# A decoder step on one core: the next step's keys transposed ahead of a step's exponential, with three slots for the memory tokens

## The chip, the cores and the metric

The kernel runs on one core of a Trainium2 chip. The metric is the device time of one execution in microseconds; lower is better. The engines are named as in the profile: PE (TensorE, matrix products and transposes) with PEld (its weight loads), DVE (VectorE), ACT (ScalarE), POOL (GpSimd) and SP (SyncE, which here only issues DMAs). All numbers are float32.

## The reference, cut to what matters

One layer of a decoder is computed for a prompt of 512 tokens and a sample group of 8 sequences with 4 new tokens each. The part that the change touches is the attention of the sample group, and what runs beside it.

```
# latent attention of the sample group over a paged cache of 2048 tokens
q_lat  = einsum('bthd,chd->bthc', q_nope, w_uk)
s_past = (einsum('bthc,bkc->bhtk', q_lat, lat_past)
          + einsum('bthr,bkr->bhtk', q_rope, kr_past)) * scale
p      = softmax(concat([s_past, s_new]))
o_lat  = einsum('bhtk,bkc->bthc', p[..., :P], lat_past) + ...
o      = einsum('bthc,chd->bthd', o_lat, w_uv)

# attention of the sample group into 256 memory tokens, 4 heads
s = einsum('bthd,bmhd->bhtm', q, mem_k) * X_HEAD_DIM ** -0.5
o = einsum('bhtm,bmhd->bthd', softmax(s), mem_v)

# expert layer: 128 experts for each of 544 tokens, rows gathered from two tables
a   = gelu(einsum('cd,ckd->ck', h, peer_u[idx]))
out = einsum('ck,ckd->cd', gate * a, peer_v[idx])
```

`lat_past` and `kr_past` are gathered by `page_table`: 8 sequences with 16 pages of 128 tokens; a page is 128 KB of latents and 16 KB of rotary keys.

## The kernel before

Tokens are taken in five tiles: four of 128 prompt tokens and one with the 32 sample tokens. The first 550 us compute projections and prompt attention, and end with the expert choice of tiles 0 and 1. From then on POOL issues one indirect DMA after another: 128 rows of `peer_u`, one for each expert place of a tile, then 128 of `peer_v`, in the order u0, v0, u1, v1, u2 and so on (`gather_order`; 1088 gathers of 512 KB). Their targets are a ring of 12 buffers. DVE reduces each u row with one custom instruction (`products`), PE adds up the v rows four at a time (`weigh`). A u gather waits for the row 12 places before it to be consumed.

Beside these gathers runs the background: `sample()` (the attention of the sample group, then its memory attention) and `part(1)` (merge of the branches, output projection, expert queries for tiles 2, 3 and 4). It is cut into units, and `background_ticks()` gives each unit a place in the order of gathers. DVE runs a unit when it has consumed the row that is 4 places ahead (`LAG`). PE and ACT have no other work in u0 and u1, so they run through their units there as fast as semaphores let them; in v0 PE runs them between quads of v rows. Everything of the background has to be over on PE before it starts on v1.

The paged attention has 16 steps (`STEPS`): four sequences and two pages each, 8 pages a step. A step s is, on the engines:

- SP and POOL load its pages into slot s % 3 (`load_pages`). SP issues five pages (ten DMAs) and POOL three. From step 3 on both wait first for the products with the values of step s - 3, which read the same slot (`pv_mm`). POOL does this in its queue of gathers, in front of gather 9 + 5 s.
- PE transposes the pages (`page_turns`, L689, 18 transposes in five groups over two banks), ACT copies each group out (L1211).
- PE makes the scores (`page_scores`, L937 and L941), DVE the running maximum (`largest`, L1695 to L1703), ACT the exponential (L1388), PE the transposed probabilities (`page_probs`, L689) and the product with the pages as values (`page_values`, L975), DVE adds it to the sum (`gather_values`, L1719 and L1720).

The program order on PE before the change, three units a step:

```
page_turns(s) | page_probs(s-1), page_scores(s) | page_values(s-1)
```

and on ACT: copies of `page_turns(s)` | copy of the probabilities of s - 1 | exponential of s. DVE has `largest(s)` in the second unit and `gather_values(s-1)` in the third. The memory attention has the same form with two units for each of 8 sequences, and loads of 1 MB into two slots (`load_memory`).

`pick` on DVE chooses experts for a head pair of a tile; in u0 it runs ahead of rows 0, 32 and 64. ACT waits in its own order for a pick's result (`picked_exp`) before it goes on with the background.

Of the kernel before, what the change touches and what calls it, by code (L numbers as in the profile page):

```python
# [13 lines left out]
P = 128  # L14
# [4 lines left out]
NB = 8  # L19
# [168 lines left out]
def hybrid_step(nc, x_prompt, x_sample, cache_lat, cache_kr, state_pool, cache_mk, cache_mv, page_table,  # L188
# [8 lines left out]
    with ExitStack() as ctx:  # L197
# [101 lines left out]
        wuvs = at(181, [2, 512])  # L299
# [3 lines left out]
        smem = [at(a, [2, 2, 512]) for a in (163, 172)]  # L303
# [75 lines left out]
        ld_smem = [sem(f"ld_smem{i}") for i in range(2)]  # L379
# [35 lines left out]
        def _(sp):  # L415
# [109 lines left out]
            def load_memory(b):  # L525
                if b < 2:
                    sp.wait_ge(pv_mm, STEPS - 2 + b)
                else:
                    sp.wait_ge(mo_mm, b - 1)
                    sp.wait_ge(mt_mm, 2 * (b - 1))  # L530
                for k, src in enumerate((cache_mk, cache_mv)):
                    sp.dma_start(smem[b % 2][:, k], src[0, b].rearrange("(m p) h e -> p m (h e)", p=P)).then_inc(
                        ld_smem[b % 2], 16)

            def load_merge(g, n):
# [6 lines left out]
                elif n < 3:  # L542
                    sp.wait_ge(mo_mm, (NB - 1, NB, NB)[n])
                    sp.wait_ge(mt_mm, 2 * NB)
                else:
                    sp.wait_ge(so_mm, 1)
                    sp.wait_ge(mo_mm, NB)
# [84 lines left out]
        def _(pool):  # L632
# [10 lines left out]
            def load_pages(s):  # L643
# [4 lines left out]
                for j, k in own_pages(s)[1]:  # L648
                    n = (4 * a + j) * PAGES + g * PGRP + k
                    page = pool.value_load(pagetab[0:1, n:n + 1], min_val=0, max_val=cache_lat.shape[1] - 1)  # L650
# [7 lines left out]
            for s, (kind, p, n) in enumerate(ORDER):  # L658
# [4 lines left out]
                if (s - 9) % 5 == 0 and 2 <= (s - 9) // 5 < STEPS:  # L663
                    load_pages((s - 9) // 5)
                if s == 124:
# [20 lines left out]
        def _(pe):  # L686
# [302 lines left out]
            def mem_turns(b):  # L989
                pe.wait_ge(ld_smem[b % 2], 32 * (b // 2 + 1))  # L990
                for i in range(2):
                    if b >= 1:
                        pe.wait_ge(mt_ev, 2 * b - 1 + i)
                    for k in range(4):
                        h, m = 2 * i + k // 2, k % 2
                        last = turn(bank[:, 4 + i, k * P:(k + 1) * P],
                                    smem[b % 2][:, 0, m, h * XD:(h + 1) * XD], P)
# [27 lines left out]
            def mem_values(b):  # L1025
# [3 lines left out]
                for m in range(2):  # L1029
                    for h in range(XH):  # L1030
                        last = pe.matmul(bank[32 * h:32 * h + TS, 7, 256:256 + XD], smpT[:, m, 32 * h:32 * h + TS],
                                         smem[b % 2][:, 1, m, h * XD:(h + 1) * XD], start=(m == 0), stop=(m == 1))
                last.then_inc(mo_mm, 1)

            def sample():

                pe.wait_ge(pq_ev, QJ)
                pe.wait_ge(sc_ev, QJ)
                for s in range(STEPS + 1):
                    if s == HALVES + 1:  # L1040
                        page_out(0)
                    if s < STEPS:
                        page_turns(s)
                    yield
# [22 lines left out]
                yield  # L1067
                pe.wait_ge(bank_zero, 2)
                for n in range(NB + 2):
                    if n >= 2:  # L1070
                        mem_out(n - 2)
                    if n < NB:
                        mem_turns(n)
                    if 1 <= n <= NB:
                        mem_probs(n - 1)
                    yield
                    if n < NB:
                        mem_scores(n)
                    if 1 <= n <= NB:
# [120 lines left out]
        def _(act):  # L1200
# [152 lines left out]

            def sample():

                act.wait_ge(id_next, 2)
                for s in range(STEPS + 1):
                    a, g = s // HALVES, s % HALVES
                    if s < STEPS:
                        for u in range(5):  # L1360
                            act.wait_ge(pt_mm, 5 * s + u + 1)
                            if s >= 1:
                                act.wait_ge(ps_mm, s)
                            src = bank[:, 4 + (5 * s + u) % 2]
                            if u < 4:
                                copy(latT[:, u].rearrange("p a b -> p (a b)"), src).then_inc(pt_ev, 1)
                            else:
                                copy(ropT[:], src[:, 0:PGRP * P]).then_inc(pt_ev, 1)
                    yield
                    if s >= 1:  # L1370
# [5 lines left out]
                        copy(probT.rearrange("p a b -> p (a b)"), bank[:, 7, 0:PGRP * P]).then_inc(pp_ev, 1)  # L1376
                    yield
# [17 lines left out]
                yield  # L1395
                for n in range(NB + 2):
                    if n < NB:
                        for i in range(2):
                            act.wait_ge(mt_mm, 2 * n + i + 1)
                            if n >= 1:  # L1400
                                act.wait_ge(ms_mm, n)
# [614 lines left out]
```

## Time and profile before

| | us |
|---|---|
| median of 3 runs (2405.80 to 2407.64) | 2406.39 |
| the profiled execution's own time | 2412.29 |
| its span, first to last instruction | 2410.6 |

The engines' busy shares of the span are PE 56%, DVE 47%, POOL 45%, ACT 13%. These are averages over stages with different limits; the rows below read the stages one by one.
### The profile page before, as it was taken

The page shows a single profiled execution, that of the slowest core. Times are in us where ns is not written, and L with a number is a line of the kernel's source. Part 1 is how long each engine was busy: PE and PEld are TensorE (multiplying, and loading weights), DVE is VectorE, ACT ScalarE, POOL GpSimd, SP SyncE. Part 2 cuts the span into 40 slices and gives each one's busy share as a digit, 9 for nine tenths or more (in the row PEclk, how much of TensorE's full clock was granted, in tenths as well). Part 3 has the DMA queues.
Part 4 walks back from the last instruction along what each step waited for, and adds up shares of the span by engine and source line. Part 5 has one row for each costly group of instructions (what it writes and reads, how often), then busy time and mean ns, then how long its engine had stood idle before and what let it go on. Part 6 is the DMA issues. An engine that isn't in the chain of part 4 may idle for free.

```text
span 2410.6 us, 22105 instructions
## 1 busy us (share of the span) xinstructions
PE 1353.5 (56%) x7122; PEld 803.3 (33%) x7122; DVE 1138.8 (47%) x2797; ACT 302.5 (13%) x760; POOL 1082.1 (45%) x1182
## 2 busy tenths in 40 slices
PE   7998999894454347998743855500045510034513
PEld 5874788783232224555531611100001100001100
DVE  2104521136757743434798074078866068840060
ACT  2214520112222121001010110000000000000000
POOL 0000000005564534555466156666666676666673
PEclk9998899996776658999865876655566755567656
DMA  6212045437786979999999579999999999999996
GB/s 197 76 57 59 1 111 147 147 107 273 252 293 223 362 277 364 353 370 374 345 389 402 180 275 364 362 391 372 373 345 353 370 384 379 369 348 358 371 384 258
DMA packets 328363, 688.02 MB, mean 285 GB/s; under 512 B 39943, under 2 KB 179528, under 8 KB 328239
## 3 DMA queue, kind: packets, MB, share of 16 engines
q0 software_dynamic: 160032, 576.69, 63.6%
q1 hardware_dynamic: 168215, 109.90, 15.7%
q8 instruction: 58, 0.95, 0.2%
q14 instruction: 58, 0.48, 0.1%
HBM read 682.36 MB, written 4.18 MB: 285 GB/s over the span
## 4 chain that ended last, share of the span: by engine, by line
PE 34%; DVE 23%; issue 12%; another core or an unknown queue 11%; DMA 8%; POOL 5%; DVEq 3%; ACT 2%; SPq 2%; POOLq 0%; ACTq 0%
PE bank L693 26%; DVE arena L1883 15%; POOL arena L640 5%; DVEq L1819 3%; PE bank L1175 3%; PE bank L689 2%; DMA arena<-in_w_mla_out_dram 2%; DMA arena<-in_peer_v_dram,arena 2%; DMA arena<-in_cache_mem_v_dram 1%; DMA arena<-in_x_sample_dram 1%; PE bank L1150 1%; DMA arena<-in_w_pool_out_dram 1%; ACT arena L1211 1%; DVE arena L1826 1%
## 5 line engine op out<-in xcount | busy, mean ns | idle before, releaser
L640 POOL DMA_INDIRECT arena<-in_peer_u_dram,arena x544 | 514.9, 947 | 842.1 <-PE bank L693 548.1
L693 PE MATMUL bank<-arena 128*128 128x256 f32 (+7 forms) x2940 | 706.1, 397 | 103.1 <-issue 52.0
L640 POOL DMA_INDIRECT arena<-in_peer_v_dram,arena x544 | 516.2, 949 | 405.6 <-PE bank L1175 159.3
L1883 DVE CUSTOM_DVE_ANT_0 arena<-arena,bank 128x1024 f32<-128x1024 f32 x544 | 639.2, 1216 | 58.5 <-issue 50.8
L693 PEld LDWEIGHTS bank<-arena 128*128 128x128 f32 (+2 forms) x2940 | 539.2, 192 | 270.2 <-issue 103.5
L1175 PE MATMUL bank<-arena 128*32 128x512 f32 x2176 | 383.4, 842 | 317.5 <-DMA arena<-in_peer_v_dram,arena 251.4
L689 PE MATMUL bank<-arena 128*128 128x128 f32 (+5 forms) x774 | 150.3, 344 | 586.3 <-DVE arena L1900 367.2
L689 PEld LDWEIGHTS bank<-arena 128*128 128x128 f32 (+5 forms) x774 | 115.0, 176 | 636.2 <-DVE arena L1900 368.4
L1175 PEld LDWEIGHTS bank<-arena 128*32 128x32 f32 x2176 | 80.3, 136 | 597.9 <-issue 597.8
L1211 ACT ACTIVATE arena<-bank 128x256 f32<-128x256 f32 (+12 forms) x399 | 156.6, 428 | 505.1 <-PE bank L693 143.5
L1912 DVE TENSOR_TENSOR arena<-arena,bank 128x1024 f32<-128x1024 f32 x5 | 6.1, 1221 | 380.7 <-PE bank L1175 194.8
L1215 ACT ACTIVATE arena<-arena 128x1024 f32<-128x1024 f32 (+5 forms) x27 | 22.6, 838 | 532.8 <-DVE arena L1912 405.3
L1787 DVE TENSOR_TENSOR arena<-arena,bank 128x256 f32<-128x256 f32 (+1 forms) x32 | 14.0, 437 | 155.5 <-PE bank L693 125.3
L1430 ACT ACTIVATE arena<-bank 128x256 f32<-128x256 f32 (+1 forms) x48 | 19.1, 398 | 305.8 <-PE bank L693 209.0
L1823 DVE MAX8 arena<-arena 128x8 f32<-128x128 f32 (+1 forms) x102 | 34.5, 338 | 36.4 <-ACT arena L1211 29.0
L1485 ACT ACTIVATE arena<-arena 128x128 f32<-128x128 f32 (+1 forms) x5 | 1.5, 293 | 397.8 <-remote 397.7
L651 POOL DMA_DIRECT2D arena<-in_cache_kv_latent_dram x42 | 23.5, 560 | 60.0 <-issue 59.9
L1883 DVE DVE_READ_ACCUMULATOR2_ANT arena<- 128x1 f32 x544 | 44.4, 82 | 4.3 <-issue 4.1
L1785 DVE TENSOR_TENSOR arena<-arena,bank 128x256 f32<-128x256 f32 (+1 forms) x16 | 7.0, 438 | 81.0 <-PE bank L693 64.8
L1150 PE MATMUL bank<-arena 128*128 128x128 f32 (+1 forms) x160 | 28.7, 290 | 24.6 <-issue 23.8
L1826 DVE MAX8 arena<-arena 128x8 f32<-128x128 f32 (+1 forms) x102 | 34.6, 339 | 8.7 <-issue 1.3
L1900 DVE TENSOR_TENSOR arena<-arena 128x128 f32<-128x128 f32 (+1 forms) x5 | 1.4, 273 | 77.9 <-ACT arena L1485 68.0
(142 smaller groups left out, 777.2 us busy)
## 6 DMA issues: line engine op xcount, KB each, us to landing
arena<-in_w_in_dram SPq DMA_DIRECT2D x48, 512.0 KB
arena<-in_w_peer_q_dram SPq DMA_DIRECT2D x32, 512.0 KB
arena<-in_cache_kv_latent_dram SPq DMA_DIRECT2D x86, 128.0 KB
arena<-in_peer_u_dram,arena POOLq DMA_INDIRECT x544
arena<-in_peer_v_dram,arena POOLq DMA_INDIRECT x544
arena<-in_w_o_dram SPq DMA_DIRECT2D x8, 1024.0 KB
arena<-in_w_in_dram SPq DMA_DIRECT2D x6, 1024.0 KB
arena<-in_cache_kv_latent_dram POOLq DMA_DIRECT2D x42, 128.0 KB
```

Of the source, the lines that this page charges most:

```text
L640: pool.indirect_dma_start(out=ring[s % RING], out_offset=None, in_=table[0], in_offset=IndirectOffsetOnAxis(ap=ix, axis=0)).then_inc(land[ ...
L651: pool.dma_start(lat[i][:, j, k], cache_lat[0][DynSlice(page, 1)].rearrange("a p c -> (a p) c")).then_inc(ld_pagp[i], 16)
L689: return pe.transpose(dst, src, eye[0:n, 0:n])
L693: last = pe.matmul(dst, lhs(k), rhs(k), start=(k == 0), stop=(k == n - 1))
L1150: last = pe.matmul(bank[0:n, 6 + i % 2, t * P:(t + 1) * P], qp[:, i % 2, t * P:t * P + n], keysT[:, i % 2], start=True, stop=True)
L1175: last = pe.matmul(bank[32 * j:32 * j + 32, c], zw[:, 32 * j + i], ring[at_slot[j] % RING][:, c * 512:(c + 1) * 512], start=(i == 0), stop ...
L1211: return act.activation(dst, src, ACT.Copy, scale=scale)
L1215: link(act.activation(junk[0:r, 0:width], src, ACT.Square, accum_out=ss[0:r, col:col + 1]))
L1819: dve.drain()
L1823: step(dve.max(values[:, 0:8], source))
L1826: step(dve.max(values[:, 8:16], source))
L1883: dve.tensor_tensor_reduce(ring[s % RING], ring[s % RING], h_dot, 1.0, 0.0, ALU.mult, ALU.add, act_a[:, p % 2, k:k + 1]).then_inc(u_free, 1)
```

## The change

`page_turns(s + 1)` and its copies move into the unit between `page_scores(s)` and `page_values(s - 1)` on PE, and on ACT ahead of the exponential of step s. The same is done in the memory attention, which gets a third slot of 1 MB. `w_uv` for the sample group moves to another address and is loaded after the third memory load instead of at step 1. SP issues six pages of a step and POOL two, whose numbers POOL now reads with one load; both keep three page slots and the same wait. The units of the paged attention get 6 rows a step instead of 5, and the later units move with them: the memory attention starts at tick 113 instead of 96, the merge goes from 160 to 268 instead of 138 to 260, the last parts in u1 start 6 rows later. The first loads of the merge get their waits anew.

```
-    return (mine, []) if s < 2 else (mine[0:5], mine[5:])
+    return (mine, []) if s < 2 else (mine[0:6], mine[6:])
...
-    ticks = [u0 + 3 + 5 * i // 3 for i in range(3 * (STEPS + 1))]
-    ticks += [u0 + 90 + 2 * i for i in range(3)]
-    ticks += [u0 + 96 + 2 * i for i in range(2 * (NB + 2))]
-    ticks += [u0 + 138 + 13 * h // 5 for h in range(2 * MERGE)]
-    ticks += [u1 + 11 + 2 * r for r in range(12)]
-    ticks += [u1 + 37 + 2 * t for t in range(3)]
-    ticks += [u1 + 44 + 5 * t // 2 for t in range(3)]
-    ticks += [u1 + 52 + 3 * j for j in range(QJ + 2)]
+    ticks = [u0 + 3 + 2 * i for i in range(3 * (STEPS + 1))]
+    ticks += [u0 + 106 + 2 * i for i in range(3)]
+    ticks += [u0 + 113 + 9 * i // 4 for i in range(2 * (NB + 2))]
+    ticks += [u0 + 160 + 23 * h // 10 for h in range(2 * MERGE)]
+    ticks += [u1 + 17 + 2 * r for r in range(12)]
+    ticks += [u1 + 43 + 2 * t for t in range(3)]
+    ticks += [u1 + 50 + 5 * t // 2 for t in range(3)]
+    ticks += [u1 + 58 + 14 * j // 5 for j in range(QJ + 2)]
...
-        smem = [at(a, [2, 2, 512]) for a in (163, 172)]
+        smem = [at(a, [2, 2, 512]) for a in (163, 171, 179)]
...
             def load_memory(b):
-                if b < 2:
-                    sp.wait_ge(pv_mm, STEPS - 2 + b)
+                if b < 3:
+                    sp.wait_ge(pv_mm, (STEPS - 2, STEPS - 1, STEPS - 1)[b])
                 else:
-                    sp.wait_ge(mo_mm, b - 1)
-                    sp.wait_ge(mt_mm, 2 * (b - 1))
+                    sp.wait_ge(mo_mm, b - 2)
+                    sp.wait_ge(mt_mm, 2 * (b - 2))
...
             for s in range(STEPS):
                 load_pages(s)
-                if s == 1:
-                    sp.dma_start(wuvs[:], w_uv[0].rearrange("(k p) h e -> p k (h e)", p=P)).then_inc(ld_wuv, 16)
             for b in range(NB):
                 load_memory(b)
+                if b == 2:
+                    sp.wait_ge(ps_mm, STEPS)
+                    sp.dma_start(wuvs[:], w_uv[0].rearrange("(k p) h e -> p k (h e)", p=P)).then_inc(ld_wuv, 16)
...
-                if (s - 9) % 5 == 0 and 2 <= (s - 9) // 5 < STEPS:
-                    load_pages((s - 9) // 5)
+                if (s - 9) % 6 == 0 and 2 <= (s - 9) // 6 < STEPS:
+                    load_pages((s - 9) // 6)
...
             def sample():
...
+                page_turns(0)
                 for s in range(STEPS + 1):
                     if s == HALVES + 1:
                         page_out(0)
-                    if s < STEPS:
-                        page_turns(s)
-                    yield
                     if s >= 1:
                         page_probs(s - 1)
                     if s < STEPS:
                         page_scores(s)
+                    yield
+                    if s + 1 < STEPS:
+                        page_turns(s + 1)
                     yield
                     if s >= 1:
                         page_values(s - 1)
                     yield
...
+                mem_turns(0)
                 pe.wait_ge(bank_zero, 2)
                 for n in range(NB + 2):
                     if n >= 2:
                         mem_out(n - 2)
-                    if n < NB:
-                        mem_turns(n)
                     if 1 <= n <= NB:
                         mem_probs(n - 1)
-                    yield
                     if n < NB:
                         mem_scores(n)
+                    yield
+                    if n + 1 < NB:
+                        mem_turns(n + 1)
                     if 1 <= n <= NB:
                         mem_values(n - 1)
                     yield
...
+            def turns_out(s):
+
+                for u in range(5):
+                    act.wait_ge(pt_mm, 5 * s + u + 1)
+                    if s >= 1:
+                        act.wait_ge(ps_mm, s)
+                    src = bank[:, 4 + (5 * s + u) % 2]
+                    if u < 4:
+                        copy(latT[:, u].rearrange("p a b -> p (a b)"), src).then_inc(pt_ev, 1)
+                    else:
+                        copy(ropT[:], src[:, 0:PGRP * P]).then_inc(pt_ev, 1)
...
+                turns_out(0)
                 for s in range(STEPS + 1):
...
                         copy(probT.rearrange("p a b -> p (a b)"), bank[:, 7, 0:PGRP * P]).then_inc(pp_ev, 1)
+                    yield
+                    if s + 1 < STEPS:
+                        turns_out(s + 1)
                     yield
                     if s < STEPS:
                         act.wait_ge(ps_max, s + 1)
```

## Rows read from the trace of the kernel before

**Rows 1.** Stretches: length; each engine's busy time (instructions); PE clock, DMA share, GB/s.
```profile
595.00:808.00 213.00, 109.00 (x934) 62.49 (x926) 142.45 (x360) 53.61 (x137) 116.33 (x155) 0.72 0.79 266
808.00:910.00 102.00, 43.68 (x339) 26.14 (x343) 57.17 (x136) 20.98 (x53) 43.79 (x44) 0.60 0.85 303
910.00:1144.00 234.00, 211.03 (x1074) 122.70 (x1066) 92.77 (x308) 26.53 (x43) 123.09 (x128) 0.96 1.04 367
1144.00:1335.00 191.00, 93.01 (x336) 64.67 (x336) 159.69 (x275) 10.66 (x26) 116.64 (x122) 0.70 1.01 380
1335.00:1394.00 59.00, 53.79 (x238) 39.95 (x242) 1.87 (x9) 17.14 (x59) 2.27 (x3) 0.93 0.37 121
```

**Rows 2.** Waits of SP's queue, 550 to 860 us: total, times, longest.
```profile
SPq L514 <- PE bank L975: 45.4, 4, 20.2
```

**Rows 3.** Timeline of SP, page issues: start us, us, what.
```profile
657.41 0.33 SPq L518 DMA_DIRECT2D arena<-in_cache_kv_latent_dram  x1
...
661.55 0.33 SPq L518 DMA_DIRECT2D arena<-in_cache_kv_latent_dram  x1
662.06 0.33 SPq L521 DMA_DIRECT2D arena<-in_cache_k_rope_dram  x1
...
670.75 0.33 SPq L518 DMA_DIRECT2D arena<-in_cache_kv_latent_dram  x1
...
697.60 0.33 SPq L518 DMA_DIRECT2D arena<-in_cache_kv_latent_dram  x1
```

**Rows 4.** Timeline of PE: transposes of a step's pages, products with the values.
```profile
587.80 4.72 PE L689 MATMUL bank<-arena 128*128 128x128 f32 x20 [23.07 <-DMA arena<-in_cache_k_rope_dram]
...
655.11 1.07 PE L975 MATMUL bank<-arena 128*32 128x256 f32 x16
...
670.46 4.58 PE L689 MATMUL bank<-arena 128*128 128x128 f32 x20 [4.61 <-DMA arena<-in_cache_k_rope_dram]
...
705.74 1.09 PE L689 MATMUL bank<-arena 128*128 128x128 f32 x8
...
761.83 1.88 PE L975 MATMUL bank<-arena 128*32 128x256 f32 x16
```

**Rows 5.** Timeline of POOL: the thirteenth gather of v1.
```profile
1397.08 0.93 POOL L640 DMA_INDIRECT arena<-in_peer_v_dram,arena  x1 [59.20 <-PE bank L1175]
```

**Rows 6.** Timeline of PE: first products of expert queries of tiles 2 to 4.
```profile
1305.50 5.20 PE L693 MATMUL bank<-arena 128*128 128x288 f32 x12 [12.32 <-issue]
...
1336.63 5.96 PE L693 MATMUL bank<-arena 128*128 128x288 f32 x16 [14.39 <-issue]
...
1343.31 4.15 PE L693 MATMUL bank<-arena 128*128 128x288 f32 x16
```

**Rows 7.** Timeline of DVE: one row of u.
```profile
666.39 1.21 DVE L1883 CUSTOM_DVE_ANT_0 arena<-arena,bank 128x1024 f32<-128x1024 f32 x1
```

**Rows 8.** Timeline of ACT and PE at a pick of DVE.
```profile
649.14 0.23 ACT L1478 ACTIVATE arena<-arena 128x32 f32<-128x32 f32 x1 [20.59 <-DVE arena L1849]
...
649.90 2.92 PE L689 MATMUL bank<-arena 128*128 128x128 f32 x12 [16.12 <-ACT arena L1211]
```

**Rows 9.** Timeline of SP: memory loads one, three and four.
```profile
791.63 0.39 SPq L532 DMA_DIRECT2D arena<-in_cache_mem_k_dram  x1
...
837.10 0.37 SPq L532 DMA_DIRECT2D arena<-in_cache_mem_k_dram  x1
...
848.47 0.37 SPq L532 DMA_DIRECT2D arena<-in_cache_mem_k_dram  x1
```

**Rows 10.** Timeline of PE: last paged values, and the turns of memory load three.
```profile
805.91 1.08 PE L979 MATMUL bank<-arena 32*32 32x256 f32 x8
...
843.87 2.40 PE L689 MATMUL bank<-arena 128*128 128x128 f32 x10 [5.82 <-DMA arena<-in_cache_mem_v_dram]
```

**Rows 11.** Timeline of PE in v0: a quad of v rows, then one merge.
```profile
919.46 1.92 PE L1175 MATMUL bank<-arena 128*32 128x512 f32 x16
921.31 6.09 PE L693 MATMUL bank<-arena 128*128 128x288 f32 x24
```

More of the change, by code:

```diff
@@ L378, in hybrid_step @@
         ld_pagp = [sem(f"ld_pagp{i}") for i in range(3)]
-        ld_smem = [sem(f"ld_smem{i}") for i in range(2)]
+        ld_smem = [sem(f"ld_smem{i}") for i in range(3)]
         ld_wuv = sem("ld_wuv")
@@ L541, in load_merge @@
                     sp.wait_ge(pool_d, PG)
-                elif n < 3:
-                    sp.wait_ge(mo_mm, (NB - 1, NB, NB)[n])
+                else:
+                    sp.wait_ge(mo_mm, (NB - 1, NB, NB, NB - 2)[n])
                     sp.wait_ge(mt_mm, 2 * NB)
-                else:
-                    sp.wait_ge(so_mm, 1)
-                    sp.wait_ge(mo_mm, NB)
                 c = OFF_G + i * D + f * P
@@ L647, in load_pages @@
                     pool.wait_ge(pv_mm, s - 2)
-                for j, k in own_pages(s)[1]:
-                    n = (4 * a + j) * PAGES + g * PGRP + k
-                    page = pool.value_load(pagetab[0:1, n:n + 1], min_val=0, max_val=cache_lat.shape[1] - 1)
+                n = (4 * a + 3) * PAGES + g * PGRP
+                _, pages = nc.values_load_multi_w_load_instructions(
+                    pagetab[0:1, n:n + PGRP], engines=[mybir.EngineType.Pool], min_val=0, max_val=cache_lat.shape[1] - 1)
+                for (j, k), page in zip(own_pages(s)[1], pages):
                     pool.dma_start(lat[i][:, j, k],
@@ L662, in _ @@
                     pool.wait_ge(ld_gain, 16 * 13)
-                if (s - 9) % 5 == 0 and 2 <= (s - 9) // 5 < STEPS:
-                    load_pages((s - 9) // 5)
-                if s == 124:
+                if (s - 9) % 6 == 0 and 2 <= (s - 9) // 6 < STEPS:
+                    load_pages((s - 9) // 6)
+                if s == 130:
                     pool.wait_ge(po_mm, 2)
@@ L989, in mem_turns @@
             def mem_turns(b):
-                pe.wait_ge(ld_smem[b % 2], 32 * (b // 2 + 1))
+                pe.wait_ge(ld_smem[b % 3], 32 * (b // 3 + 1))
                 for i in range(2):
@@ L996, in mem_turns @@
                         last = turn(bank[:, 4 + i, k * P:(k + 1) * P],
-                                    smem[b % 2][:, 0, m, h * XD:(h + 1) * XD], P)
+                                    smem[b % 3][:, 0, m, h * XD:(h + 1) * XD], P)
                     last.then_inc(mt_mm, 1)
@@ L1031, in mem_values @@
                         last = pe.matmul(bank[32 * h:32 * h + TS, 7, 256:256 + XD], smpT[:, m, 32 * h:32 * h + TS],
-                                         smem[b % 2][:, 1, m, h * XD:(h + 1) * XD], start=(m == 0), stop=(m == 1))
+                                         smem[b % 3][:, 1, m, h * XD:(h + 1) * XD], start=(m == 0), stop=(m == 1))
                 last.then_inc(mo_mm, 1)
@@ L1351, in _, with mem_out @@
                         copy(dst[:, :, cols(q + 1)], bank[:, 7].rearrange("p (c n) -> p c n", c=4)).then_inc(at_xe, 1)
+            def turns_out(s):
[6 more added lines that the diff above has]
+                        copy(latT[:, u].rearrange("p a b -> p (a b)"), src).then_inc(pt_ev, 1)
+                    else:
+                        copy(ropT[:], src[:, 0:PGRP * P]).then_inc(pt_ev, 1)
+            def mem_out(n):
+                for i in range(2):
+                    act.wait_ge(mt_mm, 2 * n + i + 1)
+                    if n >= 1:
+                        act.wait_ge(ms_mm, n)
+                    copy(smT[:, 2 * i:2 * i + 2].rearrange("p a b -> p (a b)"), bank[:, 4 + i]).then_inc(mt_ev, 1)
             def sample():
                 act.wait_ge(id_next, 2)
+                turns_out(0)
                 for s in range(STEPS + 1):
                     a, g = s // HALVES, s % HALVES
[L1359 to L1369, printed above, removed]
                     if s >= 1:
@@ L1395, in sample @@
                 yield
+                mem_out(0)
                 for n in range(NB + 2):
[L1397 to L1401, printed above, removed]
-                            copy(smT[:, 2 * i:2 * i + 2].rearrange("p a b -> p (a b)"), bank[:, 4 + i]).then_inc(mt_ev, 1)
                     if 1 <= n <= NB:
@@ L1413, in sample @@
                     yield
+                    if n + 1 < NB:
+                        mem_out(n + 1)
                     if n < NB:
```

6 lines of the change are left out of this document (3 added, 3 removed).

## The prediction, made before the changed kernel was run

> **What bounds the kernel now.** I first read the stretches [rows 1]. From 1394 us on only gathers and their reductions run; the change doesn't touch them, so all it can do lies between 550 and 1394 us. There the DMA engines are full (share 1.01 and 1.04) from 910 to 1335 us. They are not full in three places: the paged attention (595 to 808 us, share 0.79), the memory attention (808 to 910, 0.85), and 59 us at the start of v1 (0.37). Against a full share of 1.03 the three lose 51, 18 and 39 us.
>
> The second view is who waits in the paged attention. SP's page loads wait for the product with the values, L975 [rows 2], and PE's transposes wait for the rotary keys that land last [rows 4]. So a step is a loop through memory: values of step s - 3 done, pages of s issued, pages landed, transposed. The period shows in SP's first issues: 657.41 and 670.75 are 13.3 us apart [rows 3]. DVE's part, five rows and two small groups, is shorter than that, and POOL, which sits in the same wait in front of every batch, stands still with its gathers. PE is not busy there (109 of 213 us) [rows 1].
>
> The third view is the start of v1: POOL stands 59.2 us [rows 5], because PE has to end the expert queries first. While gathers run, one of the 16 queries takes 31 us (1305.50 to 1336.63), waiting for its 512 KB of weights; once they have stopped it is the products' own 4.15 us and some scores [rows 6].
>
> **The change part by part.** *The order on PE.* The critical question is what stands between two releases of a page slot. Before, values of s - 1 come after the scores of s, whose pages are two batches old. Afterwards they come behind the transposes of s + 1. Pages s + 1 are issued only when the values of s - 2 are done, since there are still three slots. So from one release to the next there is now, in series and nothing beside it: release to issue, the whole landing, the transposes, the product. The landing, which before had a whole step of other work beside it, is exposed. The terms:
>
> - Release to first issue: values end at 656.18 [rows 4], SP issues at 657.41 [rows 3]: 1.2 us.
> - Issue to transposes: 657.41 to 670.46 is the longest of seven batches, 697.60 to 705.74 the shortest [rows 3, 4]; all seven are 10.1, 12.3, 13.05, 9.9, 8.1, 12.2 and 10.0 us, mean 10.8. Left out are batches that queue behind another or end in a pick.
> - SP's sixth page is two more DMAs, 0.52 us apart (661.55 and 662.06 [rows 3]): 1.0 us. POOL's third page and two of three page-number loads go; POOL's last page isn't the one that lands last, so this is worth nothing in the loop.
> - Transposes: 20 with the probabilities' two take 4.58 us [rows 4], so 18 take 4.1 us. ACT's copies run beside them, one group behind, and the product doesn't wait for the last two.
> - Product with the values: 1.07 us at the high clock, 1.88 at the low one [rows 4]; I take 1.3.
>
> Sum 18.4 us a step, against 13.3. With the lowest of each (8.1 us, 3.3 us for transposes at the high clock, as in step 2, and 1.07) it is 14.7 us; with the highest (13.05, 4.7, 1.9) 21.9 us. I take the mean, since contention is as before: six gathers a step go out behind the pages.
>
> Beside this loop DVE has 6 rows of 1.2 us [rows 7] and some 1.5 us of its own, under 9 us: hidden. If the loop were shorter than that, it would be the bound. The exponential now stands behind the copies of s + 1 on ACT; scores of s + 1 and probabilities of s wait for it, but they take 4 us of the 12 in which the next pages land: hidden too. What the move gives back (scores no longer wait for fresh transposes) lies in this shadow.
>
> *Picks.* Two picks fall into this stage. ACT waits 20.6 us for one, and PE's transposes 16.1 us behind it [rows 8]. Afterwards a part of that lies beside a landing: about 3.5 + 20.6 + 3 + 1.3 = 28.4 us for such a step, 10 more than 18.4, and some 6 for the other, in all 16 us.
>
> *The stage.* Values of step 0 come behind the transposes of steps 1 and 2, at about 600 us instead of 595.3 (step 1's pages land at 587.80 in both [rows 4]). Values of step 13 then come at 600 + 13 x 18.4 + 16 = 855 us; before, SP shows them at 791.6 [rows 9]. The last two steps have no pages to wait for: 12 us, against 15.4 before (to 807.0 [rows 10]). So the stage ends near 867 instead of 807: 60 us later, with 17 rows more of u0 consumed.
>
> *Memory attention.* The same loop, but a third slot: load of n + 1 when values of n - 2 are done, against n - 1 before. A period is 11.4 us now (837.10 to 848.47 [rows 9]), of which 6.8 us are landing [rows 9, 10] and the rest turns, scores, probabilities and values; scores and probabilities leave the loop and loads 0 to 2 are there at once. I take 0.9 us off each of five periods and 6 us at the front: 11 us saved. `w_uv` behind the third load could be late; it is needed some 8 us after the values, and 2.5 MB at 380 GB/s are 6.6 us: nothing, at worst 8 us.
>
> *Merge.* One merge (6.09 us) and its share of quads (1.92 us each) [rows 11] bind PE: 24 merges with 1.3 quads each before, 1.15 now, so 24 x 0.15 x 1.92 = 7 us less, and with a few us less of weights that land late 12 us saved.
>
> *u1.* Merge ends at tick 268 instead of 260, so 8 gathers fewer lie between it and POOL's stop: 8 x 1.4 = 11 us less. The queries start 6 rows later against the gathers, about 8.5 us, in which a third of a query (31 us each [rows 6]) would have been done: 3 us more at the end. Together 8 us saved. The stop itself stays near 60 us.
>
> **The sum.** (600 - 595.3) + 13 P + 16 - 196.3 + (12 - 15.4) - 11 - 12 - 8 = 13 P - 210, where P is the new period. P = 18.4 gives +29 us on the profiled 2412.3, so 2441; its median was 2406.4 (6 us lower), so I predict 2435 us. The change of sign lies at P = 16.2 us.
>
> **The skill.** Our row for a page batch is 8.1 to 13.05 us from first issue to landing [rows 3, 4]. The Trainium skill (DMA: Bandwidth & Descriptors, Anatomy of one DMA) gives 2.0 us plus the bytes at 436 GB/s; for the 1.18 MB of a step this would be 4.7 us. With it P would be 12.3 us and the change some 50 us faster. The trace disagrees with it here. The same page (Queues, rings and completion order) says that a DMA engine alternates between its queues packet by packet; by this a batch behind full gather queues is slowed, and the trace agrees, in step 1's pages, which POOL's undisturbed gathers held until 587.80 [rows 4].
>
> **The rivals.**
> - *Landing is quick (faster).* It decides on SP and PE: if pages come in 8.1 us as the batch of 697.60 did [rows 3], because POOL issues two pages rather than three and the DMA engines are idle at each release, P is 14.7 us and the sum -19: 2387 us. It is faster below P = 16.2, that is with a landing under 8.6 us at otherwise mean terms. One of seven batches shows that. The page's fixed cost plus bandwidth, named above, is the extreme of it.
> - *Landing is slow.* Step 1's pages, eight from SP alone, were issued from 550.85 on, and PE waited for them until 587.80 [rows 4]. If gathers crowd the six pages, P is 21.9 us or more: +75, 2481 us.
> - *The loss is absorbed.* The DMA engines have the same bytes to move and stood still 59 us at v1; the later stages could take the delay in, if PE's chain were not what ends last there. Against it: PE is what POOL waits for at v1 [rows 5], and the background reaches it later. Time about 2406.
> - *The order doesn't matter.* If before the values of s - 1 in effect ended only when pages s + 1 had landed, the old loop is as serial as the new one but for the transposes; then P is 13.3 + 1.0 + 4.1 = 18.4 us. This is the forecast's number by another way, and I hold it for part of the reason that the old period is 13.3 and not 10.5.
>
> **How the numbers follow.** Forecast (P from 16.6 to 20.5) 0.55; slow landing 0.16; quick landing 0.19; absorbed or P near 16.2: 0.10, of which 0.07 are within 0.2% (about what a measurement of this kernel tells from no change), 0.02 slower and 0.01 faster. So faster 0.20, same 0.07, slower 0.73. The range takes in most of both outer cases: P from 15.3 to 21.3 gives -11 to +67 us: 2395 to 2473. The likeliest case's own range is 2412 to 2463.
>
> **What would show it.** Right: SP's first issues of two steps 17 to 20 us apart; PE's product with the values directly behind the transposes of the next step; transposes still started by the rotary keys' DMA, with longer waits (10 of them above 6 us); POOL's wait at its page loads 5 us and more a step; DMA share of the stage under 0.7; v0 started at 870 us or later; the stop at v1 again 55 to 70 us. Wrong: page issues 13 us apart or less, or PE's waits for the rotary keys gone.

## The result, and the profile after

| | before | after |
|---|---|---|
| median, us | 2406.8 (2405.8 to 2407.64, 4 runs) | 2490.61 (2487.09 to 2498.47, 4 runs) |
| the profiled execution's own time | 2412.29 | 2487.09 |
| its span | 2410.6 | 2485.2 |

The changed kernel is slower: the ratio is 1.0353, with a 95% interval of 1.0326 to 1.038. I had forecast 2435 us with a range of 2395 to 2473. The sign is right; the loss is 84 us where I had 29, and it lies outside the range.

The same stretches as in [rows 1], in the profile after (length; busy time of each engine with its instructions; PE clock, DMA share, GB/s):

```profile
595.00:904.00 309.00, 111.20 (x918) 64.47 (x918) 155.14 (x384) 53.73 (x137) 112.17 (x139) 0.65 0.60 201
904.00:1000.00 96.00, 49.80 (x388) 24.74 (x388) 49.71 (x139) 19.92 (x48) 43.76 (x44) 0.64 0.87 319
1000.00:1240.00 240.00, 210.34 (x1069) 127.93 (x1070) 106.81 (x317) 25.19 (x47) 127.32 (x133) 0.96 1.05 368
1240.00:1408.00 168.00, 84.93 (x314) 57.61 (x312) 137.12 (x237) 10.66 (x26) 100.17 (x106) 0.71 1.01 377
1408.00:1475.00 67.00, 57.01 (x257) 40.77 (x261) 4.86 (x24) 17.40 (x59) 3.07 (x4) 0.88 0.34 114
```

The loss is in the first line. The stretch of the paged attention is 96 us longer, with the same work on PE (111 us against 109) and the DMA engines only 0.60 busy instead of 0.79. The other four stretches together are 15 us shorter (571 us against 586); their borders are not at exactly the same places of the program, so two of them are longer and two are shorter.

The waits of the stretch from 600 to 890 us (engine, line, what it waited for; total us, times, longest):

```profile
PE bank L688 <- DMA arena<-in_cache_k_rope_dram: 153.0, 12, 15.5
POOL arena L650 <- issue: 145.3, 14, 14.4
DVE arena L1730 <- PE bank L974: 105.5, 9, 16.0
```

PE's transposes wait 12.75 us (153.0 / 12) for each batch of pages. POOL and DVE stand behind the same loop. The profile names no releaser for POOL ("issue"); by the program it waits at this place, ahead of its first page, for the product with the values that frees the slot. One step in the timeline, from one first issue of SP to the next (start us, us, engine, line, what; idle time before it and what ended it):

```profile
712.37 0.33 SPq L518 DMA_DIRECT2D arena<-in_cache_kv_latent_dram  x1
...
712.81 0.58 POOL L650 DMA_DIRECT2D arena<-in_cache_kv_latent_dram  x1 [14.36 <-issue]
...
714.56 0.54 POOL L653 DMA_DIRECT2D arena<-in_cache_k_rope_dram  x1
...
715.40 1.00 POOL L638 DMA_INDIRECT arena<-in_peer_u_dram,arena  x1 [0.30 <-issue]
715.87 0.29 SPq L518 DMA_DIRECT2D arena<-in_cache_kv_latent_dram  x1
...
721.00 0.33 SPq L521 DMA_DIRECT2D arena<-in_cache_k_rope_dram  x1
721.73 0.94 POOL L638 DMA_INDIRECT arena<-in_peer_u_dram,arena  x1 [0.30 <-issue]
...
729.19 4.30 PE L688 MATMUL bank<-arena 128*128 128x128 f32 x18 [14.77 <-DMA arena<-in_cache_k_rope_dram]
...
733.41 1.61 PE L974 MATMUL bank<-arena 128*32 128x256 f32 x16
...
735.10 0.22 DVE L1730 SCALAR_TENSOR_TENSOR arena<-arena 128x1 f32<-128x1 f32 x1 [15.14 <-PE bank L974]
...
736.27 0.33 SPq L518 DMA_DIRECT2D arena<-in_cache_kv_latent_dram  x1
```

Read as a chain this is the loop of the prediction: issue, landing, transposes, values, issue. Its terms are 16.8 us of landing (712.37 to 729.19), 4.2 of transposes (to 733.41), 1.6 of values, and 1.25 until the next issue: 23.9 us. What is new is the order in the middle. POOL is through its two pages at 715.1, so its first gather goes out at 715.40, while SP still has four of its six pages to issue, from 715.87 to 721.00. The DMA part of this stretch, 712 to 736 us in 40 slices of 0.6 us, shows what follows (queues: packets, MB, share of 16 engines):

```profile
DMA  0066796096899989999999999930000000000000
...
DMA packets 2754, 4.34 MB, mean 181 GB/s; under 512 B 1120, under 2 KB 1920, under 8 KB 2752
...
q0 software_dynamic: 1024, 3.44, 41.2%
q1 hardware_dynamic: 1728, 0.89, 13.7%
```

4.34 MB go through, POOL's two pages and six gathers on one queue and SP's six pages on the other. They are at work in 25 slices, from 713.2 to 728.2 us, and only then do the transposes begin. After that the DMA engines are idle for 13 slices, 8 us: no page slot is free, and the next gathers stand behind POOL's next page loads. So the pages did not arrive ahead of the gathers; SP's queue still moves 0.30 MB, a third of its pages, after its last issue at 721.00 us, beside the gathers. The loop holds the whole 15 us of transfer.

How much of the stage's loss the later stages give back is read from three marks. Two of them are SP's first load of the merge weights and POOL's thirteenth gather of v1, after:

```profile
1003.58 0.37 SPq L547 DMA_DIRECT2D arena<-in_w_in_dram  x1
```

```profile
1474.40 0.94 POOL L638 DMA_INDIRECT arena<-in_peer_v_dram,arena  x1 [63.32 <-PE bank L1176]
```

and the first of these two before, which was not among the rows above:

```profile
906.62 0.37 SPq L550 DMA_DIRECT2D arena<-in_w_in_dram  x1
```

The third mark is the end of the last paged values, at 907.0 us after (905.94 + 1.08) and at 807.0 before [rows 10]: 100 us later. The merge weights are asked for 97.0 us later, v1's thirteenth gather 77.3 us later [rows 5], and the span is 74.6 us longer. So the memory attention won 3 us, merge and u1 together 20, and the rest 3.

### The profile page after: what moved, and what is told of

It reads as the page before. It is cut to its first block, busy times and chain, and to the rows that moved or that the text cites. A ratio compares the mean times of both kernels' runs of the same rounds, so it can differ in the third digit from the quotient of the medians.

```text
span 2485.2 us, 22076 instructions
## 1 busy us (share of the span) xinstructions
PE 1343.0 (54%) x7122; PEld 802.4 (32%) x7122; DVE 1141.5 (46%) x2797; ACT 300.3 (12%) x758; POOL 1068.6 (43%) x1154
## 4 chain that ended last, share of the span: by engine, by line
PE 32%; DVE 15%; POOL 14%; DMA 12%; issue 11%; another core or an unknown queue 8%; SPq 5%; ACT 2%; DVEq 1%; POOLq 0%; ACTq 0%
PE bank L692 23%; POOL arena L638 14%; DVE arena L1894 12%; DMA arena<-in_peer_v_dram,arena 4%; PE bank L688 3%; PE bank L1176 3%; DMA arena<-in_cache_k_rope_dram 3%; DMA arena<-in_w_mla_out_dram 2%; SPq L518 1%; SPq L514 1%; SPq L521 1%; DMA arena<-in_w_x_out_dram 1%; DMA arena<-in_peer_u_dram,arena 1%; ACT arena L1212 1%
## 5 line engine op out<-in xcount | busy, mean ns | idle before, releaser
L1176 PE MATMUL bank<-arena 128*32 128x512 f32 x2176 | 375.3, 826 | 334.5 <-DMA arena<-in_peer_v_dram,arena 234.6
L1212 ACT ACTIVATE arena<-bank 128x512 f32<-128x512 f32 (+12 forms) x399 | 158.5, 428 | 684.4 <-PE bank L688 294.8
L650 POOL DMA_DIRECT2D arena<-in_cache_kv_latent_dram x28 | 15.7, 561 | 145.5 <-issue 145.3
```

The costliest lines, as they stand in the source:

```text
L1176: last = pe.matmul(bank[32 * j:32 * j + 32, c], zw[:, 32 * j + i], ring[at_slot[j] % RING][:, c * 512:(c + 1) * 512], start=(i == 0), stop ...
L1212: return act.activation(dst, src, ACT.Copy, scale=scale)
```

## The experiments

Each was compared with the kernel before on the same chip; before's own median differs between these comparisons (2396.6 to 2406.8 us), so the ratios are what can be set beside each other. The bands of the first four expectations were reckoned from a before of about 2407 us, while before took 2398.0 us in their comparison.

**The order alone, on the kernel before** (the edit shortened, without its conditions on s).

```
 def sample():          # TensorE
+    page_turns(0)
     for s in range(STEPS + 1):
-        if s < STEPS: page_turns(s)
-        yield
         page_probs(s - 1); page_scores(s)
         yield
+        page_turns(s + 1)
+        yield
         page_values(s - 1)
         yield
```

and the same shift of the copies on ScalarE.

> The kernel before with one part of the change alone: on TensorE the transposes of step s+1 stand ahead of the values of step s-1, and on ScalarE the copies of those transposes stand ahead of the exponential. The split of the page issues (five on SP, three on Pool), the five units a step and the copies into the key memory stay as in the kernel before. Theory 1 (the order makes a serial loop: the values of a step release a cache buffer, its pages are issued, land, are transposed, and only then come the next values): one gather and one SP issue fewer stand in a step than in the changed kernel, so the landing is about 14 us and the step 20 to 21 us; the values of step 15 end near 866 us where they ended at 791.6, and the kernel takes 2460 to 2485 us. Theory 2 (it is the six gathers and six SP pages of a step that stretch it, not the order): 2405 to 2420 us.

Measured: 2451.53 us (2446.68 to 2455.59), ratio 1.0232, interval 1.0209 to 1.0254. The values of step 13 release the first memory load at 840.28 us, where they did at 791.63 before [rows 9]. Over ten batches the time from SP's first issue to the transposes is 8.0 to 13.7 us, mean 10.9; the mean step is 18.5 us. Two thirds of the loss (2.3 of 3.5%) is the order by itself, as theory 1 says; its 2460 to 2485 us fit only by the ratio (1.0232 x 2406.8 = 2463). My number for the landing, 14 us, was too high: with three pages on POOL the gathers start 4.9 us behind the first issue and SP is finished at 6.2 to 7.8 us, and the landing is what it was before (mean 10.8 in the prediction).

**The order put back, on the changed kernel.**

```
-        page_turns(s + 1)
-        yield
         page_values(s - 1)
+        page_turns(s + 1)
+        yield
         yield
```

> The changed kernel with one thing put back: on TensorE the values of step s-1 stand ahead of the transposes of step s+1 (the third unit of the order is empty). Split of issues, six units a step and the third memory slot stay as changed. Theory 1 (serial loop through the values): a buffer is released before the transposes wait for the next landing, the landing lies under a step again, the period falls from 22.4 to 14 to 15 us, and the kernel takes 2380 to 2400 us. Theory 2 (pages land together with the six gathers of a step, so the DMA queues' 15 to 17 us a step set the period whatever the order): 17.5 us a step, 2420 to 2435 us. Theory 3 (memory part or units at fault): 2480 to 2495 us, as the changed kernel.

Measured: 2400.46 us (2398.29 to 2402.49), ratio 1.0016, interval 1.0005 to 1.0026. Six pages on SP, six gathers a step, the third memory slot and ScalarE's new order are all still there, and the loss is gone, all but 0.16%. The first memory load comes at 807.91 instead of 890.38 us, and a step takes 16.0 us on the mean, or 13.6 without the two steps with a pick: theory 1. So the serial loop is necessary for the loss: moving one call on TensorE back ahead of the wait takes 3.4% away.

**Four pages on SP and four on POOL, on the changed kernel.**

```
-    return (mine, []) if s < 2 else (mine[0:6], mine[6:])
+    return (mine, []) if s < 2 else (mine[0:4], mine[4:])
```

POOL also reads its page numbers with two loads a step, one for each sequence, where the changed kernel has one.

> The changed kernel with the eight page issues of a step split four on SP and four on Pool, where it has six and two. Theory 1 (the last page's issue on SP is part of the serial loop, about 1.05 us for each page): two issues fewer on SP take 2.1 us off each of 13 steps, the period is 20.3 us and the kernel takes 2460 to 2470 us. Theory 2 (the landing is set by what the DMA queues carry, pages and six gathers, about 15 us for a step, not by when the last page is issued): no change, 2485 to 2495 us.

Measured: 2422.54 us (2420.27 to 2430.47), ratio 1.0102, interval 1.008 to 1.0124. Both theories miss: the gain on the changed kernel is 2.5% of the time before, where two SP issues were to give about 1.0%. The timeline of one step shows why:

```profile
709.85 0.33 SPq L518 DMA_DIRECT2D arena<-in_cache_kv_latent_dram  x1
...
715.42 0.53 POOL L654 DMA_DIRECT2D arena<-in_cache_k_rope_dram  x1
...
715.62 0.33 SPq L521 DMA_DIRECT2D arena<-in_cache_k_rope_dram  x1
716.26 1.00 POOL L638 DMA_INDIRECT arena<-in_peer_u_dram,arena  x1 [0.31 <-issue]
...
718.52 4.26 PE L689 MATMUL bank<-arena 128*128 128x128 f32 x18 [4.82 <-DMA arena<-in_cache_k_rope_dram]
...
725.99 0.33 SPq L518 DMA_DIRECT2D arena<-in_cache_kv_latent_dram  x1
```

All eight pages are out before the first gather, and they are there 8.7 us after the first issue, in place of 16.8. The step is 16.1 us. SP's last issue comes at 5.8 us instead of 8.6, which is less than half of that difference. So there is a third reading, which neither theory had: POOL's share of the pages is also what holds POOL's gathers back. Give it two pages and the gathers go first.

**The gathers held back, six and two kept.** This tells the third reading from "SP's six issues take longer".

```
             # SP, at the end of a step's pages
+            if s >= 2:
+                sp.sem_inc(sp_pages, 1)
             # POOL, behind its two pages
+            pool.wait_ge(sp_pages, s - 1)
```

> The changed kernel, six page issues on SP and two on Pool as changed, but Pool begins the gathers of a step only once SP has issued the last of its six pages (SP raises a semaphore, Pool waits for it behind its own two pages). Theory 1 (pages issued behind gathers land with the gathers: what stretched the landing from 8 us with four and four to 16.5 us is the order in which pages and gathers are put into the queues): the landing falls to about 11.5 us (SP's last page at +7.8 us and the 3.5 us that passed behind the last page with four and four), the step from 23 to 18 to 19 us, and the kernel takes 2425 to 2450 us, although Pool idles 5 us more in each step. Theory 2 (SP's own six issues or the amount of data set the landing): the landing stays at 15 to 17 us, 2485 to 2510 us.

Measured: 2455.49 us (2454.7 to 2459.72), ratio 1.02, interval 1.0163 to 1.0236, against 1.0353 without the hold. A step:

```profile
721.07 0.33 SPq L519 DMA_DIRECT2D arena<-in_cache_kv_latent_dram  x1
...
729.54 0.33 SPq L522 DMA_DIRECT2D arena<-in_cache_k_rope_dram  x1
730.20 1.00 POOL L641 DMA_INDIRECT arena<-in_peer_u_dram,arena  x1 [6.35 <-SPq L526]
...
731.31 4.04 PE L692 MATMUL bank<-arena 128*128 128x128 f32 x18 [6.42 <-DMA arena<-in_cache_k_rope_dram]
...
739.96 0.33 SPq L519 DMA_DIRECT2D arena<-in_cache_kv_latent_dram  x1
```

SP issues the same six pages, with its last at 8.5 us (8.6 in the changed kernel), and moves the same bytes; yet the pages are there after 10.2 us, 1.8 us behind the last issue. Over eleven batches it is 9.6 to 11.2 us, mean 10.1, against a mean of 15.6 in the changed kernel. The kernel is faster although a wait of 6.35 us was added to POOL. That is theory 1; only its total, 2425 to 2450 us, was a little too good (below). The queues show the difference too. From 721 to 724 us in the changed kernel, just behind SP's last issue, and from 730 to 731 us here, just behind the same issue (packets, MB, share of 16 engines):

```profile
q0 software_dynamic: 242, 0.87, 83.2%
q1 hardware_dynamic: 320, 0.15, 19.0%
```

```profile
q1 hardware_dynamic: 286, 0.15, 55.9%
```

The same 0.15 MB of SP's queue take 3 us beside 0.87 MB of POOL's and 1 us when POOL's queue is empty.

**Five gathers a step in place of six, on the changed kernel.** The list of units and POOL's place for the page batches are those of before (`% 5`).

> The changed kernel with the old number of units, five rows of other work and so five gathers a step where it has six; turned order, six pages on SP and the memory part as changed. Theory 1 (with six and two all gathers of a step go ahead of or between the last pages, so the landing holds them all): one gather fewer takes 1.4 us off the landing of 16.5 us and the kernel takes 2460 to 2475 us. Theory 2 (the landing is set by SP's last issue and not by the number of gathers): 2480 to 2495 us.

Measured: 2487.25 us (2480.99 to 2489.57), ratio 1.0374, interval 1.0346 to 1.0403: no difference to the changed kernel. The mean landing is 15.3 us (13 batches) against 15.6 and the mean step 21.9 against 22.4, about a third of the 1.4 us that theory 1 wanted, and the first memory load came 4.3 us earlier (886.08 against 890.38). Against that, 13 rows less were done by then, and the time is the same. This row alone fits theory 2's number but not its reason, since with the hold above SP's last issue was as late and the landing was 5 us shorter. It shows that the sixth gather isn't the cause. Between this kernel (1.0374) and the order alone (1.0232) stand only the split, with POOL's way of reading the page numbers, and the memory part; the memory part costs nothing (below), so the split is worth 1.4% here.

**The fourth corner of order and split.** Values first as above, and four and four.

> The changed kernel with the values ahead of the transposes on TensorE (as in the run before) and with four page issues on SP and four on Pool: the fourth corner of the square of order and split. Theory 1 (the split costs only because the landing is in a serial loop): with the values ahead the landing has slack, so the split makes little difference, 2390 to 2402 us against 2400 us with six and two. Theory 2 (the split costs by itself, some 5 us a step): 68 us less than with six and two, 2330 to 2345 us.

Measured: 2402.5 us (2399.0 to 2409.2), ratio 0.9982, interval 0.9963 to 1.0. The square is:

| ratio to before | six and two | four and four |
|---|---|---|
| transposes of s + 1 first | 1.0353 | 1.0102 |
| values of s - 1 first | 1.0016 | 0.9982 |

The split (with POOL's one load more of page numbers) is worth 2.5% where the landing is in the loop and 0.3% where it isn't. Theory 1.

**The number of units alone, on the kernel before.**

> The kernel before with the change's number of units alone: six rows of the other work a step where it has five, and Pool's gathers held back accordingly. Order on TensorE and ScalarE, split of issues and memory copies stay as before. Theory 1 (a sixth gather a step is hidden in the step of 13.3 us): 2395 to 2410 us, since some 17 rows are done earlier. Theory 2 (the sixth gather lengthens each landing by the 1.4 us it takes of the DMA engines, and the landing is what the step waits for): 13 steps by 1.4 us, 2415 to 2430 us.

Measured: 2412.1 us (2406.81 to 2414.61), ratio 1.0048, interval 1.0025 to 1.0072. The time lies between the two ranges; by the ratio (1.0048 x 2406.8 = 2418) it would be in theory 2's, but neither theory names what happened. Step 13's values are only 5.2 us later (first memory load at 796.85) and not 18, and the rows run ahead: v0's first gather comes at 832.8 us instead of 862.3. But v0's thirty-second gather after it comes at 935.1 against 936.3 before, so the 29 us are gone again: v rows need TensorE's products, which stand in its fixed order among the memory steps. In 833 to 935 us the DMA share is only 0.65, where it was 0.89 before:

```profile
833.00:935.00 102.00, 45.77 (x351) 22.59 (x352) 32.74 (x110) 19.33 (x49) 33.56 (x33) 0.61 0.65 237
```

and POOL's waits between 820 and 940 us name the product (total us, times, longest):

```profile
POOL arena L640 <- PE bank L1175: 59.7, 5, 23.2
```

Rows done early in the paged stage are worth nothing if the next rows can't start. Why it is 0.5% slower, and not the same, stays open.

**The split alone and the memory part alone, on the kernel before.**

> The kernel before with its split alone changed, four page issues on SP and four on Pool where it has five and three. Theory 1 (in the old order a landing has a step of slack except behind the picks, where the profile before shows waits for a landing of 39.5 us in all): those waits shrink by some 2 us each, 2385 to 2400 us. Theory 2 (no part of the landing shows at its end): 2396 to 2410 us.

> The kernel before with the memory part of the change alone: three memory slots, the transposes of memory block n+1 and their copies ahead of the exponential of block n, the value weights loaded behind the third block, merge weights requested earlier. Theory 1 (my prediction's terms: memory stage 11 us and merge 12 us shorter): 2375 to 2392 us. Theory 2 (transfers in the memory stage are bound by the DMA engines, which carry the held-back gathers too, so what is won is given back): 2398 to 2410 us.

Measured: four and four 2397.27 us (2389.67 to 2404.12), ratio 0.9968, interval 0.9945 to 0.9991; the memory part 2401.84 us (2394.54 to 2414.01), ratio 0.9983, interval 0.9961 to 1.0004. The split is a small gain. Its time lies in both ranges; what speaks for theory 1 is the trace, in which PE's waits for the rotary keys fall from 39.5 to 15.8 us (595 to 810 us). The memory part can't be told from nothing, which is theory 2's number; my 23 us for memory and merge are not there. Its trace also warns of small shifts: its first memory load comes at 776.79 us, 14.8 earlier than before, although of the paged stage only the load of `w_uv` is changed. Whether that load or the execution makes these 15 us isn't shown, so shifts of this mark by some us, as the 5.2 and 4.3 above, say little by themselves; those that carry the argument are 35 to 82 us.

**Both together, on the kernel before.**

> The kernel before with the memory part of the change and with four page issues on SP and four on Pool; order on TensorE and ScalarE and the five units a step as before. Theory 1 (the two small gains, 9 us for the split and 4 us for the memory part, lie in different stages and add up): 2388 to 2398 us. Theory 2 (what the paging stage wins is given back in the memory stage, as with the six units alone): 2398 to 2408 us.

Measured: 2384.12 us (2373.61 to 2399.8, 12 runs), ratio 0.9949, interval 0.9929 to 0.9969. The ratio is the product of the two single ones (0.9968 x 0.9983 = 0.9951), so the two gains add up, as in theory 1; the time itself is below both ranges, with a before of 2396.6 us in this comparison. This kernel beats both, by 0.5% the one before and by some 4% the changed one (0.9949 / 1.0353). It keeps the old order and the five rows.

## Why the prediction was wrong

**The loop: right.** "So from one release to the next there is now, in series and nothing beside it: release to issue, the whole landing, the transposes, the product." The timeline after shows just that, and putting the one call back removes the loss. Most signs that I had named for it came: values directly behind the transposes, twelve waits for the rotary keys, eleven of them above 6 us, a DMA share under 0.7 (0.60), v0 at 926.0 us (870 or later), a stop of 63.3 us at v1. The first sign didn't: SP's first issues of two steps were to be 17 to 20 us apart, and they are 19.8 to 24.3, mean 22.4.

**The landing term: mis-sized, and this is the step that failed.** "I take the mean, since contention is as before: six gathers a step go out behind the pages." They don't go out behind them. I counted POOL's third page as "worth nothing in the loop", because it isn't the one that lands last. Its worth was another: it kept POOL from gathering. The term was 10.8 + 1.0 us and measured 15.6 (12 batches, 11.5 to 17.1), which is 3.8 of the 4.0 us by which the step is longer than forecast. The runs give the landing by the order in the queues:

| kernel (transposes first); us from SP's first issue of a batch | first gather behind POOL's pages | SP's last issue | landing, mean (range) |
|---|---|---|---|
| four and four | 6.4 to 8.8 us | 4.6 to 6.0 us | 8.3 (7.9 to 8.7) |
| six and two, gathers held | 8.4 to 10.0 | 7.7 to 9.3 | 10.1 (9.6 to 11.2) |
| five and three | 4.9 to 6.8 | 6.2 to 7.8 | 10.9 (8.0 to 13.7) |
| six and two, five gathers | 3.0 to 5.1 | 7.7 to 9.7 | 15.3 (13.1 to 18.3) |
| six and two (the change) | 3.0 to 6.0 | 7.7 to 10.7 | 15.6 (11.5 to 17.1) |

The 18.3 us are the last batch, behind which nine gathers go out, as behind the last one of the changed kernel (15.0 us). The shortest landing of the changed kernel is the batch of 668 us, whose own gathers were late, from 6.0 us on, behind one that had been left over at 2.0 us:

```profile
668.25 0.33 SPq L518 DMA_DIRECT2D arena<-in_cache_kv_latent_dram  x1
...
674.25 1.00 POOL L638 DMA_INDIRECT arena<-in_peer_u_dram,arena  x1 [0.30 <-DVE arena L1894]
...
679.73 1.54 PE L688 MATMUL bank<-arena 128*128 128x128 f32 x6 [1.55 <-DMA arena<-in_cache_k_rope_dram]
```

The evidence for this stood in the trace before. The quickest of my seven batches, that of 697.60 [rows 3], is the one whose first gather came late, at 6.8 us and behind SP's last issue, where it came at 4.9 us, ahead of that issue, in the other six:

```profile
703.99 0.33 SPq L521 DMA_DIRECT2D arena<-in_cache_k_rope_dram  x1
704.42 1.00 POOL L640 DMA_INDIRECT arena<-in_peer_u_dram,arena  x1 [2.22 <-issue]
```

The Trainium skill's page DMA: Bandwidth & Descriptors (Queues, rings and completion order), which I had cited, says that an engine takes its queues in turn, packet by packet. The rows of the step at 712 us would go with it: the profile counts 1728 packets for 0.89 MB in SP's queue (515 bytes each) and 1024 for 3.44 MB in POOL's (3.4 KB each), so turns by such packets would give SP's pages a small part of the bytes. The page has several descriptors in a packet, and whether the profile counts the same packets isn't shown. No run here separates the size of packets from their number either, so this is a reading and not shown; shown is that the order of issue sets the landing.

**The sum with the measured terms.** 13 P - 210 had 16 us in it for the picks. The load that step 13's values release is issued at 890.38 us and the values of step 0 end at 599.7 (598.67 + 1.07), so 13 steps took 290.7 us where 13 x 18.4 + 16 = 255 were forecast from 600: 35 of the miss (13 x 3.8 = 49 for the landing, less the 16 of the picks, makes 33 of them). The last two steps took 16.6 us instead of 12, with 8 us in which PE stood before the transposes of step 15's probabilities: 5 more. The stage ended at 907 us and not at 867. With the 6 us that came less behind the stage, 29 forecast, 35, 5 and 6 make the 75 us between the two profiled executions; the medians are 84 us apart, since the profiled execution of before was 5.5 us above its median and that of after 3.5 below its own.

**The picks: wrong in place, and right in size for another landing.** With a landing of 16 us they lie beside it: the steps with a pick are 23.1 and 23.2 us long, against a mean of 22.3 for the ten others. Where the landing is short they come out: with four and four those two steps take 23.6 and 25.0 us against a mean of 16.5 for the ten others, 16 us together, the very term of the prediction. That the size fits is luck: it belongs to a landing of 8.3 us, and with the order alone, whose landing of 10.9 us is nearest to my 11.8, only one step stands out, with 23.0 us against a mean of 18.5. With the gathers held the two are 23.2 and 22.1 us against 18.7, 8 us together, which is what that kernel's total lacked.

**Behind the stage.** I had 31 us of gain and 25 came: memory 3 instead of 11, merge and u1 20 as forecast, the rest 3. The memory part run alone confirms that three slots give nothing that can be measured.

**Which rival it was.** "Landing is slow ... If gathers crowd the six pages, P is 21.9 us or more: +75, 2481 us." Measured were 22.4 us a step and +84. It had 0.16, and my range ended at P = 21.3, just below it. The step at 587.80 [rows 4] was the evidence for it and should have weighed more: there too SP's pages were out beside undisturbed gathers. I had counted from its first issue (550.85); SP's last issue for it was at 579.43 us, and from there to 587.80 it is 8.4 us, as the 8.2 in the changed kernel. The quick landing (8.1 us) is real, but it belongs to batches whose gathers come behind the last page, as the one of 697.60 and all those of four and four. That the order doesn't matter is refuted by the run with the values put first, and that later stages absorb the loss by the sum: they give back a quarter of the 100 us.

## What to carry to other kernels

Before an operation is moved ahead of a wait, write down the loop through its buffers: if a load's slot is released by something that now stands behind another load's landing, the whole landing becomes a part of every step, and most of every change of that landing then shows in the step (7.3 us less landing with four and four made the steps without a pick 5.8 us shorter). A queue's issues are also a brake on what stands behind them on the same engine; whoever moves page issues from one engine to another must look at what goes out in their place. A landing is best estimated not by the mean of the old batches but by what will be in the queues ahead of and beside the last packet.

## What the runs showed of the hardware

- Pages whose last issue stands ahead of the gathers land some 2 to 4 us behind it (last issue 8.5 us, landed 10.2; 5.8 and 8.7); pages issued among six gathers land with them, 8.2 us behind the last issue (721.00 to 729.19), with the same bytes. SP's queue moved 0.15 MB in 3 us beside 0.87 MB of gathers, and 0.15 MB in 1 us alone.
- The DMA engines moved such a mixed batch, 4.34 MB, in 15 us, 289 GB/s, where full stretches reach 368 to 377 GB/s.
- Adding a wait of 6 us a step to POOL made the changed kernel 1.5% faster (1.02 / 1.0353): its gathers had been issued ahead of and between pages on which the loop waited, and the landing fell from 15.6 to 10.1 us.
